# POOL halves every fourth unit of transposed probabilities from a plain copy of ScalarE's, and scales the output rows first in its attention program

## The chip, the cores and the metric

The kernel runs on one core of a Trainium2 chip. The metric is the time of one execution in microseconds (us) as the device measures it. PE is TensorE, ACT is ScalarE, DVE is VectorE, POOL is GpSimd and SP is SyncE, which only issues transfers here.

## The reference

One layer of a decoder block over 2048 rows of width 1024, in float32. The part that matters here is the attention branch. An indexer scores all causal keys for each query, the 256 best are kept, and eight heads of width 64 attend to them over one shared key and value head:

```
_, idx = lax.top_k(score, topk)
att = jnp.einsum('bqhd,bqkd->bhqk', qb, k_sel).astype(jnp.float32) * (HEAD_DIM ** -0.5)
att = att - slopes[None, :, None, None] * dist[:, None]
p = jax.nn.softmax(att, axis=-1).astype(v.dtype)
return jnp.einsum('bhqk,bqkd->bqhd', p, v_sel)
```

After it the two branches are gated, merged and projected, a SwiGLU network follows, and the output is `_rmsnorm(x, norm_final)`: each row is scaled by its own reciprocal root mean square and by a gain along the columns.

## The kernel before, in words

The 2048 rows are worked on in four groups g = 0 to 3 of 512 rows, each of four blocks of 128. Every group goes through a projection phase "A", an attention phase "C" and a feed-forward phase "F", in the order A0 C0 A1 F0 C1 A2 F1 C2 A3 F2 C3 F3. Each engine has one program that is written out in this order and is worked off strictly in order; semaphores connect the programs, and there is no scheduler.

Float32 products are made of pairs of `fp32r` values: a value is halved into a "high" part (rounded by the write as `fp32r`) and a "low" part (the value less the high part), and PE multiplies with both.

**The attention phase.** All keys are scored, and those that were not chosen are masked. The phase goes over 16 pairs of heads (four blocks t of queries, four pairs in each). For one pair i and each head e of it, PE writes scores into PSUM (L1519, L1520), DVE adds the mask and takes the row minimum (L1217), and ACT takes the exponential into `probs` (L793). One or two pairs later (`lag`) the probabilities are multiplied with the values. For this they must be transposed. That goes by units k of two key tiles and both heads, 128x512 for most. PE transposes a unit into one of two PSUM banks (`transposes(k)`, L1475). ACT copies it out as the high part (L780), and DVE subtracts that from the bank to get the low part (L1226). PE multiplies both with the values in `values(k)` (L1494, L1495). PE issues `transposes(k)` and then `values(k - 2)`. `transposes(k)` waits until DVE has subtracted unit k - 2, because both use the same bank. Group 1 has 56 units, group 2 has 88 and group 3 has 120. A pair has its units in two halves, and PE issues the scores of the next head ahead of each half.

Between its subtractions DVE marks the keys that the next block of queries will use: in pair i the columns u = i % 4 (512 wide) of block i // 4 + 1, in five steps (L950, L952, L957, L959, L961), one after each of the first five units of the pair. POOL makes the mask out of the marked columns (L490, L494) and DVE needs all of a block's masks before its first pair.

**POOL's program in an attention phase.** It makes the masks of block t = 1. At block t = 2 it first calls `finish_rows(g - 1)`, which scales the 512 output rows of the group before in place: four times one operation with the row's factor (L468) and one with the gain (L469), each 128x1024. Then it goes on with the masks. The factors come from POOL itself at the end of the feed-forward phase (L563 to L569), after ACT's squares of the last rows (L894). SP stores the scaled rows.

## Time and profile before

| | |
|---|---|
| time, median of three runs | 3646.43 us (3637.72, 3646.43, 3647.69) |
| time of the profiled execution | 3637.07 us |
| its span, first to last instruction | 3635.3 us |
| busy, share of the span: PE / DVE / ACT / POOL | 89% / 61% / 32% / 20% |
| attention of groups 1, 2, 3 in the trace | 1140 to 1255, 1985 to 2175, 2928 to 3175 us |
| mean granted clock of PE | 0.958 of full speed |

The busy shares are means over phases of different kinds. The change touches only the three attention phases of the fifth row, 552 us together, and the rows below are from them.

### The profile page before, as it was taken

The page shows a single profiled execution, that of the slowest core. Times are in us where ns is not written, and L with a number is a line of the kernel's source. Part 1 is how long each engine was busy: PE and PEld are TensorE (multiplying, and loading weights), DVE is VectorE, ACT ScalarE, POOL GpSimd, SP SyncE. Part 2 cuts the span into 40 slices and gives each one's busy share as a digit, 9 for nine tenths or more (in the row PEclk, how much of TensorE's full clock was granted, in tenths as well). Part 3 has the DMA queues.
Part 4 walks back from the last instruction along what each step waited for, and adds up shares of the span by engine and source line. Part 5 has one row for each costly group of instructions (what it writes and reads, how often), then busy time and mean ns, then how long its engine had stood idle before and what let it go on. Part 6 is the DMA issues. An engine that isn't in the chain of part 4 may idle for free.

```text
span 3635.3 us, 41824 instructions
## 1 busy us (share of the span) xinstructions
PE 3252.7 (89%) x15045; PEld 2658.7 (73%) x15045; DVE 2204.6 (61%) x3903; ACT 1179.7 (32%) x2023; POOL 716.5 (20%) x482
## 2 busy tenths in 40 slices
PE   6980799889998899889999789989999967889998
PEld 5860678668886788658887668865788856768886
DVE  2748827578705827579972973657999988720001
ACT  3331641242334632251111653226211145621111
POOL 3420110025766000002112300000112231002112
PEclk9995899999999999999999999999999989999999
DMA  6960465469995265435555026542455510155554
GB/s 219 310 211 0 162 254 201 160 200 290 291 289 217 98 228 198 160 122 191 196 194 194 24 91 231 197 165 93 174 195 189 200 64 6 71 208 193 190 196 168
DMA packets 177566, 640.15 MB, mean 176 GB/s; under 512 B 11293, under 2 KB 95305, under 8 KB 115560
## 3 DMA queue, kind: packets, MB, share of 16 engines
q1 hardware_dynamic: 160512, 574.66, 45.8%
q10 hardware_dynamic: 16872, 63.01, 4.5%
q8 instruction: 121, 1.98, 0.2%
q14 instruction: 61, 0.50, 0.0%
HBM read 476.14 MB, written 161.48 MB: 175 GB/s over the span
## 4 chain that ended last, share of the span: by engine, by line
PE 62%; DVE 18%; issue 13%; ACT 3%; DMA 2%; POOL 1%; DVEq 0%; ACTq 0%; SPq 0%; POOLq 0%
PE PS L1357 13%; PE PS L1328 13%; PE PS L1329 13%; PE PS L1330 13%; DVE probs L1217 3%; DVE flags L1123 2%; PE PS L1342 2%; PE PS L1343 2%; PE PS L1344 2%; DVE PT L1226 1%; DVE W L1108 1%; DVE W L1226 1%; PE PS L1475 1%; DVE ties L952 1%; PE PS L1311 1%
## 5 line engine op out<-in xcount | busy, mean ns | idle before, releaser
L1123 DVE TENSOR_SCALAR_CACHE_REDUCE flags<-W,cand 128x1408 uint8<-128x1408 f32 (+3 forms) x462 | 683.4, 1479 | 53.7 <-DVE cand L1153 39.9
L1357 PE MATMUL PS<-WS,HT 128*128 128x512 f32 x2088 | 483.4, 391 | 5.5 <-POOL WS L440 3.2
L1357 PEld LDWEIGHTS PS<-WS,HT 128*128 128x128 f32 x2088 | 394.0, 189 | 88.9 <-issue 4.0
L1328 PE MATMUL PS<-HF,WS 128*128 128x512 f32 x1072 | 419.6, 391 | 16.1 <-issue 13.8
L511 POOL TENSOR_TENSOR TMP<-TMP 128x512 f32<-128x512 f32 x88 | 113.3, 1288 | 1558.2 <-ACT TMP L862 1558.2
L1329 PE MATMUL PS<-HF,WS 128*128 128x512 f32 x1072 | 419.1, 391 | 0.0
L1330 PE MATMUL PS<-HF,WS 128*128 128x512 f32 x1072 | 418.7, 391 | 0.0
L440 POOL TENSOR_TENSOR WS<-RAW,WS 128x1024 fp32r<-128x1024 f32 x116 | 278.1, 2398 | 647.8 <-ACT WS L583 618.0
L1328 PE MATMUL PS<-HT,WS 128*128 128x512 f32 x824 | 323.9, 393 | 0.0
L1330 PE MATMUL PS<-HT,WS 128*128 128x512 f32 x824 | 320.7, 389 | 0.0
L1329 PE MATMUL PS<-HT,WS 128*128 128x512 f32 x824 | 320.6, 389 | 0.0
L1475 PE MATMUL PS<-ident,probs 128*128 128x128 f32 x1088 | 182.4, 291 | 105.4 <-DVE PT L1226 62.5
L1328 PEld LDWEIGHTS PS<-HF,WS 128*128 128x128 f32 x1072 | 202.5, 189 | 59.7 <-issue 15.1
L1293 DVE TENSOR_TENSOR attn<-PS,XR 128x1024 f32<-128x1024 f32 x16 | 18.8, 1218 | 364.2 <-PE PS L1357 364.0
L1519 PE MATMUL PS<-KH,QS 128*128 128x512 f32 (+3 forms) x320 | 132.6, 414 | 116.3 <-DVE mx L1217 82.4
L583 ACT ACTIVATE WS<-RAW 128x1024 fp32r<-128x1024 f32 x116 | 122.8, 1059 | 340.9 <-PE PS L1330 164.4
L1330 PEld LDWEIGHTS PS<-HF,WS 128*128 128x128 f32 x1072 | 202.5, 189 | 42.3
L1329 PEld LDWEIGHTS PS<-HF,WS 128*128 128x128 f32 x1072 | 202.4, 189 | 41.9
L1475 PEld LDWEIGHTS PS<-ident,probs 128*128 128x128 f32 x1088 | 130.1, 148 | 134.6 <-issue 111.0
L995 DVE SCALAR_TENSOR_TENSOR PS<-W,cw,PS 128x512 f32<-128x512 f32 x336 | 221.9, 744 | 0.0
L793 ACT ACTIVATE probs<-probs,mx 128x128 f32<-128x128 f32 (+15 forms) x128 | 153.3, 1198 | 100.7 <-DVE mx L1217 100.5
L1357 PE MATMUL PS<-W,HT 128*128 128x512 f32 x792 | 184.9, 389 | 0.0
(220 smaller groups left out, 6126.8 us busy)
## 6 DMA issues: line engine op xcount, KB each, us to landing
WS<-split_weights_scratch SPq DMA_DIRECT2D x234, 1024.0 KB, 4.8
split_weights_scratch<-WS SPq DMA_DIRECT2D x116, 1024.0 KB, 5.0
W<-split_weights_scratch SPq DMA_DIRECT2D x114, 1024.0 KB, 4.8
RAW<-in_w_in SPq DMA_DIRECT2D x34, 512.0 KB, 6.1
RAW<-in_w_ffn_gate SPq DMA_DIRECT2D x22, 512.0 KB, 6.3
RAW<-in_w_ffn_up SPq DMA_DIRECT2D x22, 512.0 KB, 6.3
RAW<-in_w_ffn_down SPq DMA_DIRECT2D x22, 512.0 KB, 5.7
W<-in_x ACTq DMA_DIRECT2D x4, 2048.0 KB, 11.9
```

Of the source, the lines that this page charges most:

```text
L440: nc.gpsimd.tensor_tensor(out=WS[:, slot, 1, :], in0=RAW[:, slot, :], in1=WS[:, slot, 0, :].bitcast(f32), op=ALU.subtract).then_inc(w_lo, 1)
L511: nc.gpsimd.tensor_tensor(out=TMP[:, s, :], in0=TMP[:, s, :], in1=TMP[:, 2 + s, :], op=ALU.mult).then_inc(h_prod, 1)
L583: nc.scalar.activation(WS[:, slot, 0, :], RAW[:, slot, :], ACT.Copy).then_inc(w_hi, 1)
L793: nc.scalar.activation(row, row, ACT.Exp, bias=mx[:, i % held, e:e + 1], scale=-1.0, accum_out=den[:, i % held, e:e + 1]).then_inc(exp_don ...
L995: nc.vector.scalar_tensor_tensor(out=TAPSUM[:, c, :], in0=GLU[:, c, ds(k0 + i, ROWS)], scalar=cw[:, c, ds(k0 + i, 1)], in1=TAPSUM[:, c, :] ...
L1123: step(nc.vector.tensor_scalar(flags[:, 0:n], SC[:, t, 0:n], cand[:, t:t + 1].bitcast(f32), 0.0, op, ALU.add, accum_out=count[:, t:t + 1]))
L1328: mm(PS[:, bank, :], wh, src[:, 0, k, :], start=k == 0, stop=False)
L1329: mm(PS[:, bank, :], wh, src[:, 1, k, :], start=False, stop=False)
L1330: ins = mm(PS[:, bank, :], wl, src[:, 0, k, :], start=False, stop=k == KD - 1)
L1357: ins = mm(PS[:, 2 * t + half, :], lhs, split(c, w_part)[:, half * 512:(half + 1) * 512], start=first and part == 0 and w_part == 0, stop= ...
L1475: ins = nc.tensor.transpose(PS[:, 4 + k % 2, (2 * a + e) * P:(2 * a + e + 1) * P], prob(g, i, e)[:, (k0 + a) * P:(k0 + a + 1) * P], ident[ ...
L1519: mm(o, lhs, KH[:, s:s + w], start=True, stop=False)
```

## The change

POOL takes over the halving of each unit k with k % 4 == 1 in groups 1 to 3 (14, 22 and 30 units, 66 in all). For such a unit ACT's copy goes, unrounded, to the place of the low part (`pt_raw`, same size and same engine as before). POOL casts it into the place of the high part and then subtracts the high part from it in place. DVE leaves the unit out. `transposes(k + 2)` then waits for ACT's copy only, and `values(k)` waits for POOL's subtraction.

POOL's program of an attention phase is written in a new order. `finish_rows(g - 1)` now stands at its start. After it the program goes over the pairs: for each i first POOL's units of pair i - lag, then the mask of the columns that are marked in pair i.

```diff
+        def pt_raw(k, end, w):
+            s = place(k, end)
+            return TMP[:, 2 * s + 1, 0:w] if s < 2 else RAW[:, s - 2, 512:512 + w]
+        def by_pool(g, k):
+            return g > 0 and k % 4 == 1
+        def halved(g, k, pool):
+            return sum(by_pool(a, b) == pool for a in range(g) for b in range(len(slots(a)[0]))) + sum(by_pool(g, b) == pool for b in range(k))
...
-                    for b in blocks(g)[1:]:
-                        if g > 0 and b % RT == 2:
-                            finish_rows(g - 1)
-                        for s, w in units(b):
-                            t = b % RT
-
-                            pool.wait_ge(marked, MASK_BASE[g] + (t - 1) * (g + 1) + s // 512 + 1)
+                    if g > 0:
+                        finish_rows(g - 1)
+                    table, at = slots(g)
+                    lag = ways(g)[1]
+                    for i in range(PAIRS + lag):
+                        for e in range(2):
+                            for k in at[i - lag, e] if i >= lag else range(0):
+                                if by_pool(g, k):
+                                    w = table[k][2] * 2 * P
+                                    p_hi, p_lo = (pt_hl(g, k, len(table), part, w) for part in range(2))
+                                    p_raw = pt_raw(k, len(table), w)
+                                    pool.wait_ge(pt_hi, PT_BASE[g] + k + 1)
+                                    nc.gpsimd.tensor_copy(p_hi, p_raw).then_inc(pool_hi, 1)
+                                    pool.wait_ge(pool_hi, halved(g, k + 1, True))
+                                    nc.gpsimd.tensor_tensor(out=p_lo, in0=p_raw, in1=p_hi.bitcast(f32),
+                                                            op=ALU.subtract).then_inc(pool_halved, 1)
+                        t, u = i // (HEADS // 2) + 1, i % (HEADS // 2)
+                        b = RT * g + t
+                        if t < RT and u < len(units(b)):
+                            s, w = units(b)[u]
+                            pool.wait_ge(marked, MASK_BASE[g] + (t - 1) * (g + 1) + u + 1)
...
-                                nc.scalar.activation(pt_hl(g, k, len(table), 0, w), PS[:, 4 + k % 2, 0:w], ACT.Copy).then_inc(pt_hi, 1)
+                                if by_pool(g, k):
+                                    dst = pt_raw(k, len(table), w)
+                                else:
+                                    dst = pt_hl(g, k, len(table), 0, w)
+                                nc.scalar.activation(dst, PS[:, 4 + k % 2, 0:w], ACT.Copy).then_inc(pt_hi, 1)
...
-                                    dve.wait_ge(pt_hi, PT_BASE[g] + k + 1)
-                                    nc.vector.tensor_tensor(out=pt_hl(g, k, len(table), 1, w), in0=PS[:, 4 + k % 2, 0:w],
-                                                            in1=pt_hl(g, k, len(table), 0, w).bitcast(f32), op=ALU.subtract).then_inc(pt_ready, 1)
+                                    if not by_pool(g, k):
+                                        dve.wait_ge(pt_hi, PT_BASE[g] + k + 1)
+                                        nc.vector.tensor_tensor(out=pt_hl(g, k, len(table), 1, w), in0=PS[:, 4 + k % 2, 0:w],
+                                                                in1=pt_hl(g, k, len(table), 0, w).bitcast(f32), op=ALU.subtract).then_inc(pt_ready, 1)
...
-                        if PT_BASE[g] + k >= 2:
-                            pe.wait_ge(pt_ready, PT_BASE[g] + k - 1)
+                        if k < 2:
+                            if g > 0:
+                                end = len(slots(g - 1)[0]) + k - 2
+                                pe.wait_ge(pt_hi, PT_BASE[g] + k - 1)
+                                pe.wait_ge(pt_ready, halved(g - 1, end + 1, False))
+                        elif by_pool(g, k - 2):
+                            pe.wait_ge(pt_hi, PT_BASE[g] + k - 1)
+                        else:
+                            pe.wait_ge(pt_ready, halved(g, k - 1, False))
...
-                        pe.wait_ge(pt_ready, PT_BASE[g] + k + 1)
+                        if by_pool(g, k):
+                            pe.wait_ge(pool_halved, halved(g, k + 1, True))
+                        else:
+                            pe.wait_ge(pt_ready, halved(g, k + 1, False))
```

The order of the instructions shows two places. The first is POOL at the start of the attention of group 1, in the kernel before. The numbered operations L563 to L569 make the row factors; `ssq` holds the factors, `attn` the output rows, `W` the marked keys and `QI` the masks. The brackets name the semaphores that a row waits for.

```order
L569 TENSOR_TENSOR ssq<-ssq 128x4 [waits pool_step]
L490 TENSOR_SCALAR W<-W 128x512 [waits keys_marked,dist_ready]
L494 TENSOR_TENSOR QI<-W,dist 128x512 [waits pool_step]
L490 TENSOR_SCALAR W<-W 128x256 [waits keys_marked]
L494 TENSOR_TENSOR QI<-W,dist 128x256 [waits pool_step]
L468 TENSOR_SCALAR attn<-attn,ssq 128x1024 [waits gain_in,f_rstd]
L469 TENSOR_TENSOR attn<-attn 128x1024 [waits pool_step]
```

The same place in the changed kernel (L482 and L483 are the row operations there, L518 and L522 the mask's, L508 and L510 the new cast and subtraction):

```order
L597 TENSOR_TENSOR ssq<-ssq 128x4 [waits pool_step]
L482 TENSOR_SCALAR attn<-attn,ssq 128x1024 [waits gain_in,f_rstd,dist_ready]
L483 TENSOR_TENSOR attn<-attn 128x1024 [waits pool_step]
...
L518 TENSOR_SCALAR W<-W 128x512 [waits keys_marked]
L522 TENSOR_TENSOR QI<-W,dist 128x512 [waits pool_step]
L518 TENSOR_SCALAR W<-W 128x256 [waits keys_marked]
L522 TENSOR_TENSOR QI<-W,dist 128x256 [waits pool_step]
L508 CAST PT<-TMP 128x512 [waits pt_hi]
L510 TENSOR_TENSOR PT<-TMP,PT 128x512 [waits pool_pt_hi]
```

The four pairs of row operations moved ahead of the masks (three of the pairs are left out in the second piece), and the first unit that POOL halves stands behind all of them. In groups 2 and 3, where `lag` is 1, one mask stands between the rows and that unit instead of two.

The second place is PE in the first half of the first transposed pair of group 3, where units 0 to 3 are transposed, before:

```order
L1475 MATMUL PS<-ident,probs 128x128 [waits pt_ready,exp_done]
L1475 MATMUL PS<-ident,probs 128x128 x3
L1494 MATMUL PS<-PT,VV 128x256 [waits pt_ready,att_done]
...
L1475 MATMUL PS<-ident,probs 128x128 [waits pt_ready,exp_done]
L1475 MATMUL PS<-ident,probs 128x128 x3
L1494 MATMUL PS<-PT,VV 128x256 [waits pt_ready]
...
L1519 MATMUL PS<-KH,QS 128x512 [waits scores_masked]
```

and after:

```order
L1515 MATMUL PS<-ident,probs 128x128 [waits pt_ready,exp_done]
L1515 MATMUL PS<-ident,probs 128x128 x3
L1537 MATMUL PS<-PT,VV 128x256 [waits pt_ready,att_done]
...
L1515 MATMUL PS<-ident,probs 128x128 [waits pt_hi,exp_done]
L1515 MATMUL PS<-ident,probs 128x128 x3
L1537 MATMUL PS<-PT,VV 128x256 [waits pool_pt_halved]
...
L1562 MATMUL PS<-KH,QS 128x512 [waits scores_masked]
```

No instruction moved on PE. The transposes of unit 3 wait for ACT instead of DVE, and the values of unit 1 wait for POOL; the scores of the next head stand right behind that wait.

## Rows read from the trace of the kernel before

In the first group the columns are the stretch, its us, the busy us of PE, PE's weight loads, DVE, ACT and POOL with their instructions, PE's granted clock, and the transfer engines' share and GB/s.

**Rows 1.** Busy time by engine in the attention phases of groups 1 to 3.

```profile
1140.00:1255.00 115.00, 90.12 (x570) 79.99 (x570) 106.54 (x215) 84.33 (x191) 36.73 (x27) 0.88 0.22 85
1985.00:2175.00 190.00, 144.67 (x923) 126.15 (x922) 160.72 (x338) 119.12 (x229) 39.46 (x33) 0.95 0.15 53
2928.00:3175.00 247.00, 192.87 (x1225) 170.01 (x1225) 208.46 (x385) 148.74 (x256) 47.00 (x39) 0.93 0.09 34
```

**Rows 2.** Waits, whole run: engine, line, releaser, us in total, times, longest.

```profile
PE PS L1475 <- DVE PT L1226: 62.5, 42, 4.2
PE PS L1475 <- DVE W L1226: 27.0, 28, 2.7
```

**Rows 3.** Timeline of POOL, group 3: start us, us, operation.

```profile
2932.50 0.20 POOL L569 TENSOR_TENSOR ssq<-ssq 128x4 f32<-128x4 f32 x1
2940.29 0.63 POOL L490 TENSOR_SCALAR W<-W 128x512 f32<-128x512 f32 x1 [7.59 <-DVE W L961]
2941.00 1.26 POOL L494 TENSOR_TENSOR QI<-W,dist 128x512 fp32r<-128x512 f32 x1
...
2979.59 2.86 POOL L468 TENSOR_SCALAR attn<-attn,ssq 128x1024 f32<-128x1024 f32 x1
...
2999.55 2.37 POOL L469 TENSOR_TENSOR attn<-attn 128x1024 f32<-128x1024 f32 x1
```

**Rows 4.** Timeline of all engines, opening of group 3.

```profile
2945.25 0.56 PE L1494 MATMUL PS<-PT,VV 128*128 128x256 f32 x1
...
2947.61 1.22 DVE L1217 CUSTOM_DVE_ANT_0 probs<-PS,QI 128x1024 f32<-128x1024 f32 x1
```

**Rows 5.** Timelines of POOL and of all engines, opening of group 2.

```profile
1993.04 0.20 POOL L569 TENSOR_TENSOR ssq<-ssq 128x4 f32<-128x4 f32 x1
...
2004.12 0.56 PE L1494 MATMUL PS<-PT,VV 128*128 128x256 f32 x1
...
2017.86 2.85 POOL L468 TENSOR_SCALAR attn<-attn,ssq 128x1024 f32<-128x1024 f32 x1
...
2036.98 2.37 POOL L469 TENSOR_TENSOR attn<-attn 128x1024 f32<-128x1024 f32 x1
```

**Rows 6.** Timelines of POOL and of all engines, opening of group 1.

```profile
1147.94 0.27 POOL L569 TENSOR_TENSOR ssq<-ssq 128x4 f32<-128x4 f32 x1
...
1154.77 0.73 POOL L494 TENSOR_TENSOR QI<-W,dist 128x256 fp32r<-128x256 f32 x1
1155.47 2.86 POOL L468 TENSOR_SCALAR attn<-attn,ssq 128x1024 f32<-128x1024 f32 x1
...
1157.41 0.36 PE L1494 MATMUL PS<-PT,VV 128*128 128x256 f32 x1
...
1175.87 2.36 POOL L469 TENSOR_TENSOR attn<-attn 128x1024 f32<-128x1024 f32 x1
```

**Rows 7.** Busy time by engine, two stretches of the opening of group 3.

```profile
2938.00:2943.00 5.00, 1.06 (x8) 0.86 (x8) 4.74 (x10) 1.46 (x4) 1.89 (x2) 1.00 0.00 0
2943.00:2946.50 3.50, 3.44 (x17) 3.47 (x18) 3.33 (x7) 1.46 (x3) 0.00 (x0) 0.55 0.02 5
```

**Rows 8.** Timelines, late pairs of group 3.

```profile
3135.03 0.60 ACT L780 ACTIVATE PT<-PS 128x512 fp32r<-128x512 f32 x1 [0.32 <-PE PS L1475]
...
3137.01 0.36 PE L1494 MATMUL PS<-PT,VV 128*128 128x256 f32 x1
...
3142.04 1.28 DVE L1226 TENSOR_TENSOR PT<-PS,PT 128x512 fp32r<-128x512 f32 x2
```

**Rows 9.** DVE's last marking step, whole run: ns min/median/max of one line.

```profile
L961 DVE SCALAR_TENSOR_TENSOR W<-W,cand,ties x38: 351/744/2822, 369.5 to 3100.8; 128x512 f32<-128x512 f32 x28, 128x384 f32<-128x384 f32 x4, 128x128 f32<-128x128 f32 x3, 128x256 f32<-128x256 f32 x3
```

**Rows 10.** Groups of DVE from 2979.5 to 3002, while POOL scales rows.

```profile
L950 DVE TENSOR_SCALAR ties<-W,cand 128x512 f16<-128x512 f32 x2 | 3.9, 1950 | 0.0
L961 DVE SCALAR_TENSOR_TENSOR W<-W,cand,ties 128x512 f32<-128x512 f32 x1 | 2.8, 2822 | 0.0
L1226 DVE TENSOR_TENSOR PT<-PS,PT 128x512 fp32r<-128x512 f32 x4 | 2.7, 687 | 0.0
```

More of the change, by code:

```diff
@@ L221, in build_block @@
         pt_psum, pt_hi, pt_ready, pt_used = sem("pt_psum"), sem("pt_hi"), sem("pt_ready"), sem("pt_used")
+        pool_hi, pool_halved = sem("pool_pt_hi"), sem("pool_pt_halved")
         rsb_ready, recip_done, pv_psum, bc_done, att_done = sem("rsb_ready"), sem("recip_done"), sem("pv_psum"), sem("bc_copied"), sem("att_done")
```

## The prediction

> **What bounds the kernel now.** I read the three attention phases first, because the change touches nothing else. The table of busy time by stretch [rows 1] shows DVE busy for 106.5 of 115 us in group 1, 160.7 of 190 in group 2 and 208.5 of 247 in group 3, and PE busy for 90, 145 and 193. Neither is full. They wait for one another in a loop: scores, DVE's minimum, ACT's exponential, transposes, copy, subtraction, values, next scores. DVE is the fuller one. The list of waits [rows 2] says where PE feels that: ahead of its transposes it waited 62.5 and 27.0 us, 89.5 us in all, for DVE's subtraction L1226. POOL is idle for most of the time (47 of 247 us busy in group 3). But POOL has one long piece, the scaling of rows: it starts at 2979.59 and ends at 2999.55 + 2.37 = 3001.92 in group 3, 22.3 us [rows 3]. Before the change nobody waits for that piece. So the question is who stands behind it once POOL's work is needed by PE.
>
> **The new wait at the opening.** PE reaches `values(1)` early in each group: at 2945.25 in group 3 [rows 4], 2004.12 in group 2 [rows 5], 1157.41 in group 1 [rows 6]. With the change this needs POOL's first subtraction, and POOL has the row scaling ahead of it. The scaling cannot begin before POOL's own factors are there, at 2932.50 + 0.20 = 2932.7 in group 3. The steps there:
> - Scaling: 22.3 us, so until 2955.0.
> - One mask, from 2940.29 to 2941.00 + 1.26 = 2942.26 before, 2.0 us: until 2957.0. DVE has marked it in time, as it did before 2940.29.
> - The first unit: a subtraction of 128x512 by POOL, which I take from the mask's second operation, 1.26 us, and a cast that no row shows. Its bounds are L490, also one operation on one 128x512 tile, 0.63, and half of L468, which takes 2.86 for 128x1024, so 1.43 [rows 3]. I take 0.65, because L490 has no scalar read from memory and a cast has none either. With two gaps of 0.05 the unit is 2.0 us: until 2959.0.
>
> PE's wait is then 2959.0 - 2945.25 = **13.8 us**. Group 2 in the same way: factors at 1993.24, scaling 2036.98 + 2.37 - 2017.86 = 21.5, mask 2.0, unit 2.0, ready at 2018.7; wait 2018.7 - 2004.12 = **14.6** [rows 5]. Group 1 has two masks ahead of the unit, of 2.0 and 1.2 us (the second is 256 wide: 0.73 for its later operation, and 0.5 for the earlier one and the gap): factors at 1148.21, scaling 1175.87 + 2.36 - 1155.47 = 22.8, ready at 1176.2, wait **18.8** [rows 6]. Together 47.2 us.
>
> Queued behind PE's wait are the scores of the next head; behind those are DVE's next minimum, its subtractions and ACT's next exponentials. DVE and ACT have little to do meanwhile. DVE's minimum after `values(1)` started at 2947.61 [rows 4], and its scores had been there for about 0.3 us; in groups 2 and 1 that lag is about 0.8 and 0.5. Only these 1.6 us come back. DVE's marking steps meet the scaling in this stretch and are slowed, but DVE has 13 us of slack there, so I cost that at nothing. If it were no cover, it would be about 0.8 us (worked out below) for each of nine steps. The transposes of unit 3 start earlier than before, since they wait for ACT only; that gains nothing, because PE then merely reaches the same wait sooner.
>
> PE comes back slow. Between 2938 and 2943 it was busy for 1.06 of 5 us, and in the 3.5 us after that its granted clock was 0.55 of full speed, close to the lower of its two levels (1.2 against 2.4 GHz) [rows 7]. The values' matmul took 0.56 us there [rows 4] and 0.36 late in the group [rows 8]. The new wait is idle time of the same kind, so I add 0.2 us for each of 8 matmuls until the next minimum can start, 1.6 a group, 4.8.
>
> **What the earlier scaling gives back.** While POOL scaled, DVE's marking steps took longer: in group 3 L961 took 2.82 us [rows 10] against a median of 0.74 [rows 9], and the two L950 took 3.9 together. DVE's L1226, which reads one operand from PSUM, kept its 0.69 [rows 10]. Summed over the 18 steps in the three scaling stretches, each against the median of its line (6.6, 1.4 and 5.7 us over them in groups 1, 2 and 3, the rows named being the longest of group 3) it is 13.7 us, 0.76 a step. It now falls into PE's wait. DVE is the bound there for most of it; I take two thirds, 9.1 us gained.
>
> The Trainium skill ("SBUF — State Buffer", on the doors into SBUF and their contention) says that DVE and GpSimd share a port pair as an exclusive lock, held for a whole instruction, and that a DVE operation with two SBUF inputs takes part against a GpSimd operation that reads SBUF. The trace agrees, with L961 at 2.82 us beside a 2.4 to 3 us POOL operation and L1226 at 0.69. The rule speaks against this change: cast and subtraction are both such holders. It has a case of its own among the rivals.
>
> **What POOL's units give in the steady part.** L1226 follows itself at 0.60 us (two in 1.28, the second of 0.68) [rows 8]. 66 units leave DVE, 39.6 us. Counted in the program, 33 of them (2, 11 and 20 in groups 1 to 3) stand in pairs in which DVE also marks, and there DVE's order sets the pace: 33 x 0.60 = 19.8 us. The other 33 stand in pairs without marks. There PE waits for the first subtraction after the minimum, and the removed one is mostly a later one, so nothing comes of it. Against this, POOL's 2.0 us of work beside marks costs. If every second one of the 33 units makes one step wait for 0.76 us, that is 12.5 us. Net -7.3. Bounds: 0 and 39.6 for the gain, 0 and 33 x 1.26 = 42 for the contention.
>
> ACT's copies keep size and number, and no DMA or queue entry is added. SP stores the rows of the group before earlier, and nobody waits for that until the merge.
>
> **Sum.** 47.2 - 1.6 + 4.8 - 9.1 - 7.3 = **+34.0 us**. On the profiled execution, 3637.07 us with its span of 3635.3, this gives 3671. The median shown is 3646.43, 9.4 above it. The four times known fall in two pairs (3637.07 and 3637.72; 3646.43 and 3647.69), so I add the sum to their middle, 3642: **3676 us**. Under 0.3%, 11 us, a measurement cannot be told from no change.
>
> **The rivals.**
> - *POOL is late in the steady part as well* (slower still). ACT's copy of a second unit ended at 3135.63 and PE took its values at 3137.01 [rows 8]. POOL would be done at about 3137.8, 0.8 us late, with the scores queued behind it. If the 33 units without marks each cost 0.8 (26 us) and contention eats the relief of the others (7.3 lost), it is +34.0 + 7.3 + 26 = +67, 3709. Against it: in other halves PE comes to `values(k)` more than 2 us after the copy, because it still waits for DVE.
> - *Every POOL unit blocks a mark* (slower still). Each of the 33 units in marking pairs makes one step wait for the whole subtraction, 1.26 us, 42 us instead of 12.5: +34.0 + 29 = +63, 3705. L961 with 2.1 us over its median [rows 9, 10] speaks for it; against it, the mean over 18 steps was 0.76 while POOL never paused.
> - *DVE's relief is paid in full* (no change). If DVE set the pace everywhere, all 39.6 and all 13.7 us would count: 47.2 - 1.6 + 4.8 - 39.6 - 13.7 = -3, 3639. The 93% of group 1 speak for it; the 84% of groups 2 and 3 against [rows 1].
> - *Faster: the loop is loosened.* Transposes of a later unit wait for ACT only after a POOL unit. If a quarter of the 89.5 us [rows 2] comes back on top of the case before, -3 - 22 = -25, 3617. It decides from the point where relief and loosening together pass 50.4 + 11 = 61 us, more than the 39.6 that leave DVE. It lacks any sign that the opening wait is covered.
>
> **How the numbers follow.** My case 0.72, POOL late throughout 0.10, every unit blocking 0.04, paid in full 0.08, loosened 0.06. My case alone reaches from +18 (contention half of what I took, three quarters of the relief counted) to +50 (cast at 1.43, no net relief in the steady part, colder PE): 3660 to 3692. For 8 in 10 I take 3655 to 3705, which holds my case and the nearer part of the first two rivals. Slower by over 0.3%: 0.85; within 0.3%: 0.09; faster: 0.06.
>
> **What would show it.** In the profile after, the waits must name a wait of PE's L1537 for POOL's L510 with three long ones of 13 to 19 us, and the phases of groups 1 to 3 must be longer by about 15, 12 and 7 us (each one's share of the terms above). The cast should take 0.6 to 0.7 us. Marking steps should be slower than their medians between the pairs, not only in the opening. L1515's wait for DVE should fall below 89.5. I am wrong if those three waits are short, which would mean that PE comes to unit 1 later or that the scaling runs faster alone, or if the late pairs of group 3, which have no marks, get longer or shorter by more than 1 us each.

## The result and the profile after

The changed kernel took **3681.91 us** (median of 4, 3680.93 to 3684.13) beside 3646.37 us (median of 4, 3637.72 to 3647.69): ratio 1.0102, 95% interval 1.0086 to 1.0118, **slower by 1.0%**, 35.5 us. The forecast was 3676 us in a range of 3655 to 3705.

The attention phases in the trace, from the first operation of POOL's factors (L591, before the change L563) to VectorE's last low part of the attention rows (L1283, before L1250), here and in the experiments below. All are in us, and each is one profiled execution. How far two traces differ without a reason in the edit can be read from the rest of the span, which no edit below touches: it took 3093.3 us before, 3101.4 after, and 3093.4 to 3103.7 in the experiments.

| | group 1 | group 2 | group 3 | sum |
|---|---|---|---|---|
| before | 115.2 | 181.1 | 245.7 | 542.0 |
| after | 131.1 | 195.0 | 252.5 | 578.6 |
| difference | +15.9 | +13.9 | +6.8 | +36.6 |

The forecast had 15, 12 and 7 here. The two traced executions lie 44.8 us apart (3637.07 and 3681.89), 36.6 in these phases and some 8 in the rest of the span; the medians are 35.5 apart, since the traced execution before was one of the quick ones. The first fence is the page's part 1, the second three rows of the list of waits of the changed kernel, whole run (us in total, times, longest), which answer to [rows 2].

```profile
PE 3261.6 (89%) x15045; PEld 2668.2 (73%) x15045; DVE 2188.5 (59%) x3837; ACT 1180.8 (32%) x2023; POOL 837.1 (23%) x614
```

```profile
PE PS L1537 <- POOL PT L510: 58.1, 27, 13.3
PE PS L1515 <- DVE PT L1259: 41.9, 27, 7.8
PE PS L1515 <- DVE W L1259: 25.9, 24, 3.0
```

TensorE's wait for VectorE's subtraction fell from 89.5 to 67.8 us, and a new one of 58.1 us stands beside it. The same list, cut to the opening of each group (1146 to 1180, 2010 to 2044, 2966 to 3000), gives for the new wait:

```profile
PE PS L1537 <- POOL PT L510: 13.3, 1, 13.3
...
PE PS L1537 <- POOL PT L510: 11.2, 1, 11.2
...
PE PS L1537 <- POOL PT L510: 7.8, 1, 7.8
PE PS L1515 <- DVE PT L1259: 7.8, 1, 7.8
```

So 32.3 of the 58.1 us are one wait in each group. What it waits for is in POOL's timeline of group 1 (start, us, operation), with TensorE's row after it; they answer to [rows 6]:

```profile
1150.65 2.86 POOL L482 TENSOR_SCALAR attn<-attn,ssq 128x1024 f32<-128x1024 f32 x1 [0.17 <-issue]
...
1169.45 2.34 POOL L483 TENSOR_TENSOR attn<-attn 128x1024 f32<-128x1024 f32 x1
1171.88 0.62 POOL L518 TENSOR_SCALAR W<-W 128x512 f32<-128x512 f32 x1
1172.59 1.26 POOL L522 TENSOR_TENSOR QI<-W,dist 128x512 fp32r<-128x512 f32 x1
1173.94 0.41 POOL L518 TENSOR_SCALAR W<-W 128x256 f32<-128x256 f32 x1
1174.44 0.72 POOL L522 TENSOR_TENSOR QI<-W,dist 128x256 fp32r<-128x256 f32 x1
1175.11 0.61 POOL L508 CAST PT<-TMP 128x512 fp32r<-128x512 f32 x1
1175.80 1.26 POOL L510 TENSOR_TENSOR PT<-TMP,PT 128x512 fp32r<-128x512 f32 x1
...
1177.12 0.58 PE L1537 MATMUL PS<-PT,VV 128*128 128x256 f32 x1 [13.28 <-POOL PT L510]
```

The scaling runs without a gap from 1150.65 to 1171.8, the masks of two marked ranges follow, then the cast and the subtraction, and 0.06 us later TensorE goes on. The three such matmuls stand 30.2, 28.7 and 29.1 us after the start of POOL's factors, against 13.0, 13.5 and 15.2 before the change: 17.2, 15.2 and 13.9 us later, 46.3 together. The waits for POOL in them are only 13.3, 11.2 and 7.8. The other 3.9, 4.0 and 6.1 us TensorE lost before it came to these matmuls.

In group 3 the forecast wait of 13.8 us is split in two in the rows above, 7.8 for VectorE and then 7.8 for POOL. VectorE's marks meet the scaling there and hold its first subtraction back; TensorE would have stood in front of POOL anyway. TensorE's clock is in the windows of that place (stretch, its us, busy us of PE, its weight loads, DVE, ACT and POOL, granted clock):

```profile
2984.00:2995.00 11.00, 2.79 (x12) 2.42 (x12) 7.63 (x11) 2.86 (x4) 10.66 (x7) 0.50 0.24 96
2995.40:2999.00 3.60, 3.59 (x11) 3.01 (x12) 0.62 (x1) 0.00 (x0) 0.00 (x0) 0.50 0.00 0
2999.00:3004.00 5.00, 5.00 (x31) 4.57 (x30) 3.43 (x8) 3.29 (x6) 1.80 (x2) 0.85 0.00 0
```

After a stretch with 2.79 of 11 us busy, TensorE worked its first 3.6 us at a granted clock of 0.50, the lower of its levels (1.2 GHz of 2.4).

Where the pairs stand tells the rest. VectorE's reciprocal of the second pair of a group, counted from POOL's factors, starts 18.2, 16.7 and 14.7 us later than before the change, 49.6 together; that of the last pair 14.4, 14.2 and 6.7, 35.3 together. So 14.3 us come back between the second pair and the last. The pairs 12 to 15 of group 3, which have no marks, kept their length: the distance to the times before the change stays at 6.7 to 7.0 us over them.

Two of the 24 smaller waits for POOL are long, 5.1 and 4.6 us, both in group 1. The second one, with ScalarE's copy, POOL's timeline and TensorE's row:

```profile
1216.16 0.58 ACT L812 ACTIVATE TMP<-PS 128x512 f32<-128x512 f32 x1
1218.76 0.62 POOL L518 TENSOR_SCALAR W<-W 128x512 f32<-128x512 f32 x1 [8.34 <-DVE W L993]
1219.46 1.27 POOL L522 TENSOR_TENSOR QI<-W,dist 128x512 fp32r<-128x512 f32 x1
1220.67 0.81 POOL L508 CAST PT<-TMP 128x512 fp32r<-128x512 f32 x1
...
1222.97 0.55 PE L1537 MATMUL PS<-PT,VV 128*128 128x256 f32 x1 [4.55 <-POOL PT L510]
```

ScalarE's copy was there at 1216.74 and POOL had been idle for 8.34 us, but in POOL's program the unit stands behind a mask, and the mask waits for VectorE's last mark of the pair. The cast begins 3.9 us after the copy. So a unit can be late although POOL has nothing to do.

### The profile page after: what moved, and what is told of

Read it like the earlier page. It is cut to its first block and busy times, and to the rows that moved or that the text cites. A ratio compares the mean times of both kernels' runs of the same rounds, so it can differ in the third digit from the quotient of the medians.

```text
span 3680.0 us, 41890 instructions
## 1 busy us (share of the span) xinstructions
PE 3261.6 (89%) x15045; PEld 2668.2 (73%) x15045; DVE 2188.5 (59%) x3837; ACT 1180.8 (32%) x2023; POOL 837.1 (23%) x614
## 5 line engine op out<-in xcount | busy, mean ns | idle before, releaser
L1361 PE MATMUL PS<-HF,WS 128*128 128x512 f32 x1072 | 420.7, 392 | 16.0 <-issue 13.8
```

What stands on the lines that cost most here:

```text
L1361: mm(PS[:, bank, :], wh, src[:, 0, k, :], start=k == 0, stop=False)
```

## The experiments

All ratios are against the kernel before, run on the same chip beside each variant (medians 3640 to 3643 us), so 0.0010 is 3.6 us. All edits are to the changed kernel. Which units go to POOL is the one line in `by_pool`.

### Where the loss is: scaling first alone, and POOL units only later

**Scaling first, no POOL units.** Half of the change by itself: POOL scales first in its attention program, and VectorE subtracts everywhere.

```diff
         def by_pool(g, k):
-            return g > 0 and k % 4 == 1
+            return False
```

> The scaling of rows stands first in POOL's attention program, and POOL halves no unit. My theory: nobody waits for the scaling, so the opening wait of 47 us is gone. The collisions of the scaling with DVE's marks only move to the opening, where PE does not wait for POOL and they are now uncovered: about nine steps of 0.76 us there against the 13.7 us that go. Change against the kernel before: -7 to 0 us, -3 likeliest. Rival A (the two thirds of the collisions that I booked as gained are gained by the move alone): -9 us. Rival B (the early scaling itself costs PE at the opening, through DVE's delayed first subtraction): +3 to +10 us.

Measured: 3655.53 us, ratio **1.0045** (1.0031 to 1.0058). The move of the scaling costs 16 us by itself, where −7 to 0 was expected; rival B (+3 to +10) has the sign. The trace shows only part of it: it is of the quickest of the five executions (3644.86 us at a mean granted clock of 0.958), and the other four took 3653.1 to 3660.0 at 0.952 to 0.955, without a trace. In it the second pairs are 4.0, 5.3 and 7.8 us later than before the change (17.1), and the last pairs 3.4, 3.5 and −2.0 us (4.9), so 12.2 come back. VectorE's marking steps in the three phases (the five, and the copy of one column between them) take 108.9 us in this trace and 109.0 in the one before: the collisions moved and did not shrink. What is late in the openings is in VectorE's groups of the opening of group 3 (2937.8 to 2963: busy us, mean ns), where POOL scales:

```profile
L991 DVE SCALAR_TENSOR_TENSOR ties<-W,cand,ties 128x512 f16<-128x512 f32 x2 | 5.1, 2530 | 0.0
...
L982 DVE TENSOR_SCALAR ties<-W,cand 128x512 f16<-128x512 f32 x2 | 2.9, 1442 | 0.0
...
L984 DVE TENSOR_TENSOR_SCAN ties<-ties 128x512 f16<-128x512 f16 x1 | 2.0, 2020 | 0.0
...
L993 DVE SCALAR_TENSOR_TENSOR W<-W,cand,ties 128x512 f32<-128x512 f32 x1 | 1.5, 1487 | 0.0
```

The same steps in the opening of the kernel before (2930 to 2955), where POOL does not scale:

```profile
L959 DVE SCALAR_TENSOR_TENSOR ties<-W,cand,ties 128x512 f16<-128x512 f32 x2 | 1.5, 748 | 0.0
L961 DVE SCALAR_TENSOR_TENSOR W<-W,cand,ties 128x512 f32<-128x512 f32 x2 | 1.5, 746 | 0.0
...
L952 DVE TENSOR_TENSOR_SCAN ties<-ties 128x512 f16<-128x512 f16 x1 | 1.2, 1226 | 0.0
L950 DVE TENSOR_SCALAR ties<-W,cand 128x512 f16<-128x512 f32 x2 | 1.0, 482 | 0.0
```

2 x 1.78 + 2 x 0.96 + 0.79 + 0.74 = 7.0 us of stretch in the four kinds of steps, and the second pair is 7.8 us late. Without POOL's units nothing covers them: the marks stand ahead of VectorE's subtractions, for which TensorE waits. The expectation set nine stretched steps against the 13.7 us for all three openings; nine are in this one opening.

**POOL units only from the fifth pair on** (51 of 66).

```diff
-            return g > 0 and k % 4 == 1
+            return g > 0 and k % 4 == 1 and slots(g)[0][k][0] >= 4
```

> As the changed kernel, but POOL's units start with the fifth pair of each group (51 of 66 units), when the scaling is over. My theory (the loss is the opening wait): at or below the kernel before, -10 to 0 us, -6 likeliest, so 40 us below the changed kernel; no wait of PE for POOL above 2 us. Rival (POOL is late in the steady part too): +15 us or more against before, with PE's wait for POOL's subtraction above 20 us in sum.

Measured: 3652.45 us, **1.0035** (1.0021 to 1.0048). Leaving out the 15 first units takes 29 us off the changed kernel's 1.0102 (0.0067, 24 us, by the ratios, which compare on the same chips). They are a quarter of POOL's units and two thirds of the loss. The other 51, against the run above, are worth 0.0010, within the measurement's uncertainty of 0.0019. The expectation of −10 to 0 us was missed (+13), mostly by the 16 us of the run above; TensorE also waited 21.4 us for POOL in 21 waits, up to 4.5, where none above 2 was expected.

**The 51 units in two parts**: the 21 in pairs in which VectorE also marks, and the 30 in pairs without marks.

```diff
-            return g > 0 and k % 4 == 1
+            return (g > 0 and k % 4 == 1 and slots(g)[0][k][0] >= 4 and (slots(g)[0][k][0] + ways(g)[1]) < 12
+                    and (slots(g)[0][k][0] + ways(g)[1]) % 4 <= g)
```

The other part has `not (...)` around the last two conditions.

> As the kernel with late units, but only those 21 of them that stand in pairs in which DVE marks. By my terms a unit relieves DVE by 0.60 us and costs half a collision of 0.76: -0.22 us each, -5 us against the kernel with the scaling first and no units. Rival (every unit blocks a marking step for the whole of POOL's subtraction): +0.66 each, +14 us. Rival (relief in full, no collision): -13 us.

> As the kernel with late units, but only those 30 of them that stand in pairs in which DVE does not mark. My theory: 0 against the kernel with the scaling first and no units, within 2 us, since PE waits there for another subtraction. Rival (POOL is 0.8 us late on each, with the scores behind it): +24 us, or +12 where half of them are late. Rival (DVE's relief counts in full): -18 us.

Measured: 1.0034 (1.0022 to 1.0046) and 1.0036 (1.0022 to 1.0050). Neither can be told from the run without POOL units (1.0045) or from the one with all 51. The intervals are too wide to say which part brings anything. They are narrow enough against the rivals: relative to the scaling first, +14 and −13 us were their values for the first part and +24, +12 and −18 for the second, and measured are −4 and −3, each with an uncertainty of 7.

### What the units' part is made of

The units in the steady part of a phase do three things: they free VectorE, they stretch its marking steps, and they are ready later. Four runs take them apart, all with the scaling first, on the same 51 units.

**Relief alone.** Nobody makes the low part of these units, and TensorE multiplies the high part twice.

```diff
-                            p_hi, p_lo = (pt_hl(g, k, len(table), part, 4 * P)[:, a * 2 * P:(a + 1) * 2 * P] for part in range(2))
+                            p_hi, p_lo = (pt_hl(g, k, len(table), 0 if by_pool(g, k) else part, 4 * P)[:, a * 2 * P:(a + 1) * 2 * P]
+                                          for part in range(2))
```

> The scaling first, as in the run with no POOL units. In the 51 units of pairs 4 and later that POOL would halve, nobody makes the low part: VectorE leaves the subtraction out, POOL does nothing, and TensorE multiplies the high part twice in its place (the same number of matmuls, an output that is only rounded more coarsely). Against the run with the scaling first and no POOL units (1.0045): theory A (VectorE's time is on the path in the steady part, and POOL's contention took the relief back): 51 x 0.6 = 31 us of relief, of which 12 to 20 show, 1.0000 (0.9985 to 1.0015). Theory B (there was never a relief, because what TensorE waits for is another chain than VectorE's busy time): 1.0045 within 0.0012.

Measured: 3636.26 us, **0.9986** (0.9977 to 0.9995): 0.0059, 21.5 us, better than the scaling first alone. Theory A by its size: leaving work out does shorten the phases. Here TensorE also waits for no low part of these units, and its transposes of unit k + 2 wait for ScalarE's copy only.

**Contention alone.** VectorE subtracts everywhere; POOL does the pair of operations besides, on other data.

```diff
+                                if shadow(g, k):
...
+                                    nc.gpsimd.tensor_copy(scratch, dist[:, 0:w]).then_inc(pool_hi, 1)
+                                    pool.wait_ge(pool_hi, done[0])
+                                    nc.gpsimd.tensor_tensor(out=scratch, in0=dist[:, 0:w], in1=scratch.bitcast(f32),
+                                                            op=ALU.subtract).then_inc(pool_halved, 1)
```

> The scaling first. VectorE halves all units as in the kernel before, and POOL does a cast and a subtraction of the same shape for each of the 51 late units besides, on other data into a place that nobody reads. Against the run with the scaling first and no POOL units (1.0045): theory A (POOL's two-operand work on SBUF lengthens VectorE's marks, 12.5 us by my sum): 1.008 (1.0065 to 1.0095). Theory B (no cost of contention): 1.0045 within 0.0012. If the run without low parts gains as much as this one loses, the two make up the nothing that the late units were worth.

Measured: 3664.46 us, **1.0065** (1.0051 to 1.0079), 0.0020 or 7.3 us worse than the scaling first alone, with an uncertainty of 0.0019, so hardly clear of noise. Theory A's sign at its lower end. VectorE's marking steps in the phases take 117.5 us here against 108.9. Relief and contention together would be −0.0039, and the real units gave −0.0010, so something was missing.

**Contention and a wait.** As the last, and TensorE's value products of these units wait for POOL as well.

```diff
+                        if shadow(g, k) or g > 0 and k == len(table) - 1:
+                            pe.wait_ge(pool_halved, sum(shadow(a, b) for a in range(g) for b in range(len(slots(a)[0])))
+                                       + sum(shadow(g, b) for b in range(k + 1)))
```

> As the run in which POOL does a cast and a subtraction for each of the 51 late units besides VectorE's own, on data that nobody reads (1.0065), but here TensorE's value products of such a unit also wait until POOL has done its pair, as they would if POOL made the low part. The three runs before it give, against the scaling first without POOL units (1.0045): relief alone -0.0059, contention alone +0.0020, both and POOL's lateness together (the 51 late units) -0.0010. Theory A (the missing +0.0029, 11 us, is lateness: POOL has its unit ready 1.2 us or so after VectorE would): 1.0065 + 0.0029 = 1.0094 (1.0080 to 1.0110). Theory B (lateness costs nothing, relief and contention merely don't add): 1.0065 within 0.0013.

Measured: 3670.12 us, **1.0067** (1.0054 to 1.0081). Theory A had 0.0029 for the wait and 0.0002 was measured, with an uncertainty of 0.0019: added to VectorE's own subtraction, the wait for POOL costs nothing that can be measured. TensorE waited 12.0 us on it, 17 times, in place of other waits.

**Relief and a wait.** That run left a gap, though: in it VectorE's subtraction had to be waited for anyway. In the run with relief alone, TensorE was also spared every wait for a low part.

```diff
+                                    nc.gpsimd.iota(GAIN[:, 0:w], pattern=[[1, w]], base=0, channel_multiplier=-1,
+                                                   allow_small_or_imprecise_dtypes=True).then_inc(pool_hi, 1)
...
-                            pe.wait_ge(pt_hi, PT_BASE[g] + k + 1)
+                            pe.wait_ge(pool_halved, halved(g, k + 1, True))
```

> As the run without low parts in the 51 late units (VectorE leaves the subtraction out, TensorE multiplies the high part twice; 0.9986), but the value products of such a unit also wait until POOL has written two ramps of 128x1024 numbers, which read nothing from SBUF and take about the 2 us of a cast and a subtraction. The wait of TensorE on both VectorE and POOL cost nothing (1.0067 against 1.0065), but there VectorE's own subtraction had to be waited for anyway; the run without low parts was spared that wait too, a gain that no POOL unit can give. Theory A (a good part of its 21 us against the scaling first was that spared wait): 1.0018 to 1.0035, and TensorE waits some 15 to 25 us for POOL. Theory B (its gain was VectorE's freed time, and POOL's contention on SBUF takes it back in the real units): 0.9986 within 0.0012, POOL's waits covered.

Measured: 3648.82 us, **1.0019** (1.0010 to 1.0028): 0.0033, 12 us, of the 21.5 were that spared wait. As with POOL's real units, it is not all slowness of POOL: the longest, 4.7 us, is again one behind a mask that waits for VectorE's mark. POOL's group and TensorE's wait in this run:

```profile
L509 POOL IOTA attn<- 128x1024 f32 x49 | 49.1, 1003 | 185.3 <-ACT PT L811 185.3
L512 POOL IOTA attn<- 128x1024 f32 x49 | 49.0, 999 | 3.3
```

```profile
PE PS L1514 <- DVE PT L1258: 51.2, 34, 7.3
...
PE PS L1514 <- DVE W L1258: 21.0, 18, 2.6
PE PS L1537 <- POOL attn L512: 20.2, 23, 4.7
```

Two ramps are 2.0 us, as long as a cast and a subtraction. The sum now closes: 1.0045 for the scaling first, −0.0059 for no subtraction at all, +0.0033 for waiting until POOL would be ready, +0.0016 that remains to the real units' 1.0035, close to the 0.0020 that contention cost by itself. The uncertainties are 0.0016 for the relief, 0.0013 for the wait, 0.0019 for the contention and 0.0016 for the remainder, and all but the second rest on the five executions of the scaling first or of the late units. So relief and wait are shown; contention is just at the edge of the noise in both places, and its size is not shown.

### Putting the pieces elsewhere

**Scaling behind the last mask, no POOL units.**

```diff
-                    if g > 0:
-                        finish_rows(g - 1)
...
+                        if g > 0 and i == 8 + g:
+                            finish_rows(g - 1)
```

> No POOL units; POOL scales the output rows in one block of about 20 us after the group's last mask, when VectorE has no marks left in the group, instead of between its masks as the kernel before does. Theory A (the marks' collisions with the scaling, 13.7 us of stretched marks in the kernel before, are on the path, since the run with the scaling first lost 17 us in the openings by them): the attention programs get 9 to 14 us shorter than the kernel before's, ratio 0.9965 (0.9955 to 0.9980). Theory B (stretched marks are covered unless they stand in the opening): no change, 1.0000 (0.9985 to 1.0012). Theory C (the rows' stores, now later in SyncE's queue, hold a load behind them): over 1.002, with a wait of TensorE on a DMA that the kernel before has not.

Measured: 3633.71 us, **0.9979** (0.9970 to 0.9988), faster than both kernels. The phases are 110.0, 179.6 and 241.0 us, 530.6 together, 11.4 below the kernel before. Two marking lines (ns min/median/max), which answer to [rows 9]:

```profile
L991 DVE SCALAR_TENSOR_TENSOR ties<-W,cand,ties x38: 352/743/752, 370.5 to 3092.2; 128x512 f16<-128x512 f32 x28, 128x384 f16<-128x384 f32 x4, 128x128 f16<-128x128 f32 x3, 128x256 f16<-128x256 f32 x3
L993 DVE SCALAR_TENSOR_TENSOR W<-W,cand,ties x38: 350/744/752, 371.2 to 3096.0; 128x512 f32<-128x512 f32 x28, 128x384 f32<-128x384 f32 x4, 128x128 f32<-128x128 f32 x3, 128x256 f32<-128x256 f32 x3
```

The longest L993 is 0.752 us, where the line before the change had one of 2.822. The marking steps take 94.8 us in the phases, 14.2 less than before, close to the 13.7 that the prediction read from single rows. The expectation had 9 to 14 us; the phases gave 11.4 and the medians 7.6.

**All 66 POOL units from the first on, scaling behind the last mask in single steps.**

```diff
+                                    for _ in range(2 if g == 1 else 1):
+                                        if i > 8 + g and rows_done < 2 * RT:
+                                            finish_step(g - 1, rows_done)
+                                            rows_done += 1
```

> All 66 POOL units, from the first of each group on; the scaling of the rows goes behind the group's last mask, one operation after each later POOL unit (two in the first of the three groups), so that no unit waits for more than one or two of them. Theory A (the wait of the first units behind the scaling was the loss): the opening waits fall from 32 us to about 3 each 1 us, ratio 0.999 (0.9965 to 1.0015) beside 1.0102 for the changed kernel. Theory B (POOL's units are slow by themselves wherever they stand: cast and subtraction 1.9 us against VectorE's 0.7, behind masks too): 1.005 or more, with TensorE waiting for POOL in the openings although nothing is scaled there.

Measured: 3637.60 us, **0.9990** (0.9981 to 0.9999), theory A: with every POOL unit in place, and only the scaling away from them, the loss of 1.0% is gone. The waits of TensorE in it:

```profile
PE PS L1551 <- POOL PT L520: 36.0, 27, 5.1
PE PS L1529 <- DVE PT L1273: 33.6, 29, 3.4
...
PE PS L1529 <- DVE W L1273: 24.8, 22, 3.0
```

and in the run without POOL units, with the scaling at the same place:

```profile
PE PS L1515 <- DVE PT L1259: 54.6, 40, 3.4
PE PS L1515 <- DVE W L1259: 26.4, 27, 2.7
```

81.0 us of waits for VectorE became 58.4, and 36.0 for POOL came beside them: 94.4. The units exchange one wait for another.

**All 66 units, one scaling operation behind each of the group's first eight.** Here the scaling is in the opening again, but no unit has the whole of it ahead.

```diff
+                                    if rows_done < 2 * RT:
+                                        finish_step(g - 1, rows_done)
+                                        rows_done += 1
```

> All 66 POOL units from the first on; the scaling is spread over the group's first eight POOL units, one operation behind each, so a unit waits for 2.3 to 2.9 us of scaling at most, but the scaling again meets the marks of the opening. Theory A (the wait behind the block of scaling is the loss, the collisions with marks a smaller part): 0.999 of the run with the scaling behind the last mask, plus the collisions that the kernel before has as well (0.0021): 1.001 (0.9990 to 1.0035). Theory B (only keeping the scaling out of the marks' way brought the time back): near 1.0045 or above.

Measured: 3645.0 us, **1.0004** (0.9996 to 1.0013), as theory A had it. Taking the block apart is worth 0.0098 by itself; moving its pieces away from the marks as well, another 0.0014, with an uncertainty of 0.0012.

**Scaling behind the last mask, POOL units only behind that.** The expectation gives the number of units as 28; counted in the program it is 19 (5, 6 and 8).

```diff
-            return g > 0 and k % 4 == 1
+            return g > 0 and k % 4 == 1 and slots(g)[0][k][0] + ways(g)[1] >= 13
```

> A candidate: the scaling in one block behind the last mask (0.9979), and POOL units only from two or three pairs behind it on (28 of the 66), where POOL has nothing else and VectorE no marks. Theory A (a POOL unit trades VectorE's 0.6 us for its own lateness wherever TensorE waits for the low part): no change against 0.9979, within 0.0012. Theory B (units away from marks and scaling bring relief without contention): 0.9960 to 0.9968.

Measured: 3638.92 us, **0.9988** (0.9979 to 0.9998). Not theory B; it is 0.0009, 3 us, behind the same kernel without units, and that difference is inside the uncertainty. In group 1 the scaling was not yet over when the first of them was due (POOL's timeline):

```profile
1230.11 2.35 POOL L483 TENSOR_TENSOR attn<-attn 128x1024 f32<-128x1024 f32 x1
1232.41 0.61 POOL L506 CAST PT<-TMP 128x512 fp32r<-128x512 f32 x1
1233.10 1.26 POOL L508 TENSOR_TENSOR PT<-TMP,PT 128x512 fp32r<-128x512 f32 x1
```

TensorE waited 4.5 us for it, so this run is no clean test of quiet units. In groups 2 and 3, with 14 of the 19 units, the phases were 177.4 and 242.4 us beside 179.6 and 241.0 without units: no sign of a gain there either.

## Why the prediction was right

**The opening waits** (47.2 us) were the step that carried it, and they came out: POOL's path ahead of the first unit was put together from rows of the same operations, and the value products stand 46.3 us later. As waits they are shorter than the 13 to 19 us that were to be seen (13.3, 11.2, 7.8): the prediction named "PE comes to unit 1 later" as a sign of being wrong, and PE did come later, by 14.0 us in all, held up by the stretched marks. Since POOL is the later of the two, the sum did not change. The cast, of which no row existed, took 0.61 us against 0.65 assumed. That these waits are the loss is shown twice: without the first 15 units two thirds of it go, and with all units but the scaling taken apart or moved, all of it.

**Lag and slow clock** (−1.6 and +4.8) made 50.4 us at the second pair; 49.6 were measured. That is 3.3 more than the 46.3, beside the forecast 3.2.

**Marks in the opening, costed at nothing.** Right for the changed kernel, and only for it. The stretched marks showed up as TensorE waiting 7.8 us for VectorE before it waited for POOL, and POOL would have been the later one anyway. With that cover gone they cost 17.1 us at the second pairs. The bound that the prediction set beside the zero, 0.8 us for each of nine steps, 7.2, is what group 3 alone lost (7.8); for three openings it was too small.

**The give-back** (−9.1). Without POOL units 12.2 us came back after the second pair, and with no collisions with the scaling at all the kernel gained 7.6 to 11.4 us. Two thirds of the 13.7 us of collisions was a good choice. In the changed kernel 14.3 us came back where this term and the next one make 16.4.

**The steady part** (−7.3) is where the working was wrong, although the sum hid it. The runs are of the 51 late units. By the prediction's own terms, with 21 of them in pairs with marks, these have 12.6 us of relief (21 x 0.60) and 8.0 of contention (10.5 x 0.76), net −4.6. The runs give three terms: 21.5 us when nothing is subtracted and nothing waited for, 12 us back for the time until POOL is ready, and 6 to 7 for contention; what remains is 3.6 us with an uncertainty of 7, and next to the better place of the scaling, nothing (+0.0011). The failed step is the one that gave POOL's lateness to the first rival alone ("POOL is late in the steady part as well"), as a mishap on top, instead of a term of the likeliest case. It put the wait at nothing and 12 us were measured. The relief was set too low by 9 us, which nearly paid for it, and that is luck. Contention was about right in size, as far as the runs can tell.

**The first rival** had 33 waits of 0.8 us in pairs without marks, 26 us. The 24 waits beside the three of the openings are 58.1 − 32.3 = 25.8 us, but that is chance: 13 of them, 8.1 us, are in pairs without marks. The other 11, 17.6 us, are in pairs with marks, and 9.6 of these are the two in group 1 that stand behind a mask.

**The other rivals.** "Every POOL unit blocks a mark" would be 26 us for the 21 units with marks and falls with the 7 us of contention. That POOL stretches marks between the pairs was to be seen, and was: the marking steps take 125.6 us in the three phases, against 109.0 before. "Relief paid in full" would be 30.6 us for the 51 units and falls with the 21.5 us that even no subtraction at all gave. "The loop is loosened" found its wait shortened (89.5 to 67.8 us, as forecast below 89.5), but not the time.

**The base.** The sum was added to 3642, the middle of the times then known. The median before is 3646.37, so 4.4 of the 5.9 us between 3676 and 3681.91 come from there; the change itself was forecast at +34.0 and measured at 35.5.

**The group sums** (15, 12 and 7 against 15.9, 13.9 and 6.8) held.

What stays open: whether units away from marks are worth anything by themselves. Their 0.0009 is inside the uncertainty, and the run meant to settle it had a wait of its own. No run put a unit ahead of the mask that waits for VectorE's mark, so what that order costs was not measured apart. How the cost of contention arises was not settled either: the run with contention alone was 15.5 us longer in its attention phases than the scaling first alone (562.4 against 546.9), but that compares it with the trace that is 10.7 us quicker than its median. The marks' stretch of 8.6 us is of the size of the 7.3 us by the medians; in the run with contention and a wait it was 17.5 us for the same time, so it is not paid one to one. The granted clock of the profiled run with contention was 0.950 against 0.958, and its share was not separated.

## What to carry to other kernels

Before work is handed to an idle engine, read what that engine already has at the moment when the first piece is due: a block of 21 us that nobody waits for becomes a wait as soon as something with a reader stands behind it. With all units on POOL, the kernel was 1.0% slower with the block ahead of them and as fast as before with its operations between them; without any unit on POOL, the block behind the last step that it stretches gave 0.2%. And freed time on the fuller engine has to be charged with how much later the new engine is ready: here 12 of 21 us went back that way. Part of that lateness can be the order of the new engine's own program, where a piece that is ready stands behind one that waits.

## What the runs showed of the hardware

- How POOL's operations stretch VectorE's depends on which. The four kinds of marking steps shown took 1.44 to 2.53 us on the mean while POOL scaled, against 0.48 to 1.23, and the step with a single SBUF tensor and a scalar of one column from SBUF (L982, 0.48) was among them, at 1.44; VectorE's subtraction from PSUM stayed at 0.69 throughout. The Trainium skill ("SBUF — State Buffer", "Who interferes with whom") names two kinds of VectorE operations: those with two SBUF inputs, against a GpSimd operation that reads SBUF, and those in a 2-port mode, which a `tensor_scalar` can enter. The stretch of L982 fits the second kind: undisturbed it takes 0.48 us for 128x512 where the steps with two inputs take 0.75. No run here tested which mode it was in.
- On POOL a cast of 128x512 from f32 to fp32r is 0.61 us and a subtraction of the same size 1.26 to 1.29. Scaling 128x1024 by a column of SBUF is 2.85, more than the product of two such tensors (2.40).
- After the opening wait TensorE's granted clock was 0.50 over the next 3.6 us of solid work, and 0.85 over the 5 us after them.
